# A third of a wide projection moved into the mLSTM cell, in steps between the cell's own matmuls

## The reference, cut to what matters

```python
proj = x @ w_in                      # (512, 1024) @ (1024, 4*768 + 12 + 256)
q, k, v = heads of proj[:, 0:768], proj[:, 768:1536] * 128**-0.5, proj[:, 1536:2304]
o_gate  = proj[:, 2304:3072]
# per head and chunk c (128 positions), with the state before the chunk:
s   = (q @ k.T) * exp(d - m)                       # 128 x 128, causal
num = s @ v + w_inter * (q @ c_prev)               # and den likewise
h   = num / max(|den|, exp(-m))
c_new = decay * c_prev + (w * k).T @ v
h   = (h - mean) * rsqrt(var + eps) * norm_g       # per head
out = sigmoid(o_gate) * h
y   = concat([out, h_mem]) @ w_out                 # then LayerNorm, router, experts
```

## Time and profile before

| | us |
|---|---|
| time, median of 3 | 1474.45 |
| the profiled execution, its own time | 1475.07 |
| its span | 1473.1 |
| PE busy (matmul) | 1350.9, 92% |
| PE weight loads | 724.1, 49% |
| DVE busy | 504.1, 34% |
| ACT busy | 287.8, 20% |
| mLSTM cell | from 866.3 to 932.4 |

### The profile page before, as it was taken

One profiled execution on the slowest core, in us unless ns is written; L12 is line 12 of the kernel. 1 busy time (PEld: TensorE's weight loads), 2 busy tenths in 40 slices (PEclk: granted clock), 3 DMA queues, 4 the chain that ended last, 5 costly groups with the idle time before them and its releaser, 6 DMA issues. The chain is left out here.

```text
span 1473.1 us, 16175 instructions
## 1 busy us (share of the span) xinstructions
PE 1350.9 (92%) x6590; PEld 724.1 (49%) x6590; DVE 504.1 (34%) x1042; ACT 287.8 (20%) x507; POOL 39.1 (3%) x64
## 2 busy tenths in 40 slices
PE   6999899999999899988999986698999999989885
PEld 5878683333333333325677875585333333333331
DVE  3264683123122122123543328575122122121221
ACT  3231340011011011012532212431011011010111
POOL 1000000000000000000000000000000000000000
PEclk9999999999999999999999998799999999999998
DMA  8320759999999999997133042249999999999994
GB/s 361 157 86 1 318 209 420 426 428 428 427 425 427 427 428 427 428 427 291 58 115 115 0 189 97 86 160 406 427 427 427 427 427 427 427 427 428 428 427 185
DMA packets 39628, 465.85 MB, mean 316 GB/s; under 512 B 6400, under 2 KB 6528, under 8 KB 12160
## 3 DMA queue, kind: packets, MB, share of 16 engines
q1 hardware_dynamic: 34656, 455.33, 73.6%
q0 software_dynamic: 4608, 8.40, 1.5%
q10 hardware_dynamic: 288, 1.05, 0.2%
HBM read 460.55 MB, written 12.58 MB: 321 GB/s over the span
## 5 line engine op out<-in xcount | busy, mean ns | idle before, releaser
L1054 PE MATMUL bank<-ring,xT 128*64 128x512 f32 x2048 | 460.4, 596 | 44.7 <-DMA ring<-in_w_pack 44.4
L1054 PEld LDWEIGHTS bank<-ring,xT 128*64 128x64 f32 x2048 | 149.0, 137 | 311.5 <-issue 311.2
L1093 PE MATMUL bank<-ring,pad 128*64 128x512 f32 x1024 | 237.7, 606 | 7.1 <-DVE pad L1275 3.2
L1265 DVE COPY xT<-bank 128x512 f32<-128x512 f32 x60 | 41.5, 691 | 442.5 <-PE bank L1040 442.5
L1093 PEld LDWEIGHTS bank<-ring,pad 128*64 128x64 f32 x1024 | 69.2, 138 | 165.7 <-issue 152.8
L1186 ACT ACTIVATE pad<-bank 128x256 f32<-128x256 f32 x64 | 24.5, 383 | 460.0 <-PE bank L1054 460.0
L1192 ACT COPY pad<-bank 128x512 f32<-128x512 f32 x64 | 37.4, 585 | 346.3 <-PE bank L1093 346.3
L1275 DVE COPY pad<-bank 128x256 f32<-128x256 f32 x64 | 27.0, 423 | 179.7 <-PE bank L1068 179.7
L1040 PEld LDWEIGHTS bank<-x_sb 128*128 128x128 f32 x480 | 58.1, 191 | 49.0 <-issue 45.4
L451 PE MATMUL bank<-x_half_hi,w_half_hi 128*128 128x512 f32 x160 | 64.0, 400 | 11.5 <-DVE x_half_lo L506 11.5
L1110 PE MATMUL bank<-pad,x_sb 64*128 64x512 f32 x256 | 72.3, 641 | 1.4 <-ACT pad L1192 1.4
(11 more groups left out here) (264 smaller groups left out, 1436.7 us busy)
## 6 DMA issues: line engine op xcount, KB each, us to landing
ring<-in_w_pack SPq DMA_DIRECT2D x190, 2048.0 KB, 35.0
ring<-in_mlstm_w_in SPq DMA_DIRECT2D x6, 2048.0 KB, 7.3
ring<-in_conv_slabs SPq DMA_DIRECT2D x6, 1536.0 KB, 10.2
ring<-in_w_out SPq DMA_DIRECT2D x2, 4096.0 KB, 12.3
ring<-in_w_kv_mem SPq DMA_DIRECT2D x2, 2048.0 KB, 26.2
ring<-in_w_pack SPq DMA_DIRECT2D x4, 1024.0 KB, 41.0
x_rows<-x_sb SPq DMA_DIRECT2D x6, 512.0 KB, 2.6
ring<-in_xT SPq DMA_DIRECT2D x4, 512.0 KB, 8.3
```

The lines of the kernel that those rows point to most:

```text
L1054: last = nc.tensor.matmul(GU_BANK[e % 2][64 * f:64 * f + 64, :], xgT[e // 2 % 2][:, 4 * h + c, 64 * (e % 2):64 * (e % 2) + 64], gu[:, c, f ...
L1093: last = nc.tensor.matmul(Y_BANK[e % 2][64 * n:64 * n + 64, :], hidT[e % 2][:, c, 64 * f:64 * f + 64], dn[:, f, c, 512 * n:512 * n + 512], ...
L1265: V.tensor_copy(xgT[q % 2][:, 4 * h:4 * h + 4, :], o[:, :].rearrange("p (c r) -> p c r", c=4)).then_inc(xcopied, 1)
```

## The change

The third group of wide pieces (8 to 11) leaves the projection's script. The pieces 8 to 10 are still split there, by ACT and DVE, into the four places; the last, piece 11, is split at the start of the cell. The cell then computes the 512 gate columns tile by tile: the tile of chunk c in eight steps of three matmuls into bank 7, put at hand-chosen places between the cell's own matmuls (`open_gates(n)` issues the next n steps; 6 + 5 + 9 + 8 + 4 over the stretches before chunk 0 and in chunks 0 to 3), and ACT takes the Sigmoid of each finished tile. Since bank 7 is taken, the state product and the turned output use bank 6 alone, three heads at a time, and the second three wait until the first three are read. x's high half must live through the cell, so the working tiles move from xT to R0. w_out's place holds x's low half and split weights, so its load waits for the last step; of the experts' units only one is loaded in the cell, behind the last raw weights, and units 1 and 2 follow with unit 3 after the cell.

```diff
-EARLY = (0, 3)
+EARLY = (0, 1)
...
-                flat = xT[:, :, :].rearrange("p k s -> p (k s)")
-                cell = lambda i, n: flat[:, i * 784:i * 784 + ML_HEADS * n].rearrange("p (h d) -> p h d", h=ML_HEADS)
+                cell = lambda i, n: R0[:, 4096 + i * 784:4096 + i * 784 + ML_HEADS * n].rearrange("p (h d) -> p h d", h=ML_HEADS)
...
-                script += [("wide", i) for i in range(2, 12)]
+                script += [("wide", i) for i in range(2, 8)]
                 pieces = [st for st in script if st[0] not in ("S", "T", "V", "cols")]
+                pieces += [("wide", i) for i in range(8, 12)]
+                IN_CELL = len(pieces) - 1
...
-                    if st in pieces and pieces.index(st) + 3 < len(pieces):
+                    if st in pieces and pieces.index(st) + 3 < IN_CELL:
...
                 @block.sync
                 def _(sp):
-                    sp.dma_start(w_out_sb, w_out[1]).then_inc(in_w_out[1], 16)
+                    sp.wait_ge(w_lo, 1)
                     for n in range(EARLY[1]):
                         load_unit(sp, 1, n)
+                    sp.wait_ge(o_done, N_CHUNKS)
+                    sp.dma_start(w_out_sb, w_out[1]).then_inc(in_w_out[1], 16)
...
+                    def open_gates(n):
+                        for _ in range(n):
+                            c, k = o_steps.pop(0)
+                            if c and k == 0:
+                                pe.wait_ge(o_out, c)
+                            if c == 0 and k == 6:
+                                pe.wait_ge(w_lo, 1)
+                            hi, lo = (by_2(a)[:, k % 2, :] for a in o_half[k // 2])
+                            z = slice(c * P, (c + 1) * P)
+                            for w, xh in ((hi, x_hi), (hi, x_lo), (lo, x_hi)):
+                                last = nc.tensor.matmul(bank[7][:, :], xh[:, k, z], w, start=(k == 0 and w is hi and xh is x_hi),
+                                                        stop=(k == KT - 1 and w is lo))
+                            if k == KT - 1:
+                                last.then_inc(o_done, 1)
...
                         last.then_inc(spread, 1)
+                        open_gates(fill[0])
...
                         last.then_inc(scored, 1)
+                        open_gates(fill[1])
...
+                    def turn_out(c, fill):
                         pe.wait_ge(h_ready, c + 1)
+                        for i in range(2):
+                            if i == 0 and c < N_CHUNKS - 1:
+                                pe.wait_ge(inter_read, 2 * c + 2)
+                            else:
+                                pe.wait_ge(h_out, 2 * c + i)
+                            for j in range(3):
+                                last = nc.tensor.transpose(third(P)[:, j, :], hh[:, 3 * i + j, :], ident[:, :])
+                            last.then_inc(h_turned, 1)
+                            if i == 0:
+                                open_gates(fill)
+
+                    front(0, (0, 2))
+                    open_gates(4)
...
+                            for i in range(2):
+                                if i:
+                                    pe.wait_ge(inter_read, 2 * c - 1)
+                                elif c > 1:
+                                    pe.wait_ge(h_out, 2 * (c - 1))
+                                for j in range(3):
+                                    last = nc.tensor.matmul(third(HD)[:, j, :], qT[:, 3 * i + j, z], state[:, 3 * i + j, :],
+                                                            start=True, stop=True)
+                                last.then_inc(inter, 1)
+                                if i == 0:
+                                    open_gates(1)
...
                         if c < N_CHUNKS - 1:
-                            front(c + 1)
+                            front(c + 1, ((2, 4, 3)[c], 0))
+                            open_gates((3, 2, 2)[c])
+                        else:
+                            open_gates(3)
                         if c:
-                            turn_out(c - 1)
-                    turn_out(N_CHUNKS - 1)
+                            turn_out(c - 1, (2, 2, 0)[c - 1])
+                    turn_out(N_CHUNKS - 1, 0)
...
+                    def gate(c):
+                        act.wait_ge(o_done, c + 1)
+                        nc.scalar.activation(ogate[:, c, 256:768], bank[7][:, :], ACT.Sigmoid).then_inc(o_out, 1)
...
+                    nc.scalar.copy(by_2(o_half[3][0]), last_raw).then_inc(w_hi, 1)
                     weights(0)
                     for c in range(N_CHUNKS):
                         if c < N_CHUNKS - 1:
                             weights(c + 1)
+                        gate(c)
...
-                            dve.wait_ge(inter, c)
                             for i in range(2):
-                                last = V.tensor_tensor(three(qC, i), pair(6, HD)[i], col(c, W_COL, i, HD), ALU.mult)
-                            last.then_inc(inter_read, 1)
-                            dve.wait_ge(inter_read, c)
+                                dve.wait_ge(inter, 2 * c - 1 + i)
+                                V.tensor_tensor(three(qC, i), third(HD), col(c, W_COL, i, HD), ALU.mult).then_inc(inter_read, 1)
+                            dve.wait_ge(inter_read, 2 * c)
...
+                        dve.wait_ge(o_out, c + 1)
                         V.tensor_tensor(hh[:, :, :], hh[:, :, :], ogate[:, c, :].rearrange("p (h d) -> p h d", h=ML_HEADS),
...
                     weigh_scores(0)
+                    dve.wait_ge(w_hi, 1)
+                    V.tensor_tensor(by_2(o_half[3][1]), last_raw, by_2(o_half[3][0]), ALU.subtract).then_inc(w_lo, 1)
```

More of the change, by code:

```diff
@@ L1612, in mlstm_phase @@
                 results, ends = [], []
-                for i, (kind, n) in enumerate(pieces):
+                for i, (kind, n) in enumerate(pieces[:-4]):
                     if kind != "wide":
@@ L1619, in mlstm_phase @@
                     else:
-                        banks = ((2, 3, 4, 6), (0, 1, 5, 7), (2, 3, 4, 6))[n // 4]
-                        results += [(("v", "vo", "o")[n // 4], t, banks[t], n // 4 > 0) for t in range(TT)]
+                        banks = ((2, 3, 4, 6), (0, 1, 5, 7))[n // 4]
+                        results += [(("v", "vo")[n // 4], t, banks[t], n // 4 > 0) for t in range(TT)]
                         ends.append(ends[-1] + TT)
@@ L1626, in ended @@
                     what, n = results[m][0:2]
-                    if what in ("v", "vo", "o"):
-                        return ends[pieces.index(("wide", 4 * ("v", "vo", "o").index(what) + 3))] - TT + n + 1
+                    if what in ("v", "vo"):
+                        return ends[pieces.index(("wide", 4 * ("v", "vo").index(what) + 3))] - TT + n + 1
                     return ends[pieces.index((what, n))]
@@ L1868, in cell_phase @@
             HD = ML_DH + 1
+            last_piece, last_raw = d["split_in_cell"]
+            o_half = [w1_half[(last_piece - 3 + q) % 4] for q in range(4)]
+            by_2 = lambda a: a[:, :].rearrange("p (k n) -> p k n", k=2)
             s = lambda n: sem("p5_" + n, ph)
+            w_hi, w_lo, o_done, o_out = s("w_hi"), s("w_lo"), s("o_done"), s("o_out")
             spread, compared, exped, weighed = s("spread"), s("compared"), s("exped"), s("weighed")
@@ L1874, in cell_phase @@
             scored = s("scored")
+            third = lambda w: bank[6][:, 0:3 * w].rearrange("p (h d) -> p h d", h=3)
             pair = lambda b, w: [bank[b + i][:, 0:3 * w].rearrange("p (h d) -> p h d", h=3) for i in range(2)]
@@ L1879, in _, with front @@
                 def _(sp):
-                    sp.dma_start(w_out_sb, w_out[1]).then_inc(in_w_out[1], 16)
+                    sp.wait_ge(w_lo, 1)
                     for n in range(EARLY[1]):
                         load_unit(sp, 1, n)
+                    sp.wait_ge(o_done, N_CHUNKS)
+                    sp.dma_start(w_out_sb, w_out[1]).then_inc(in_w_out[1], 16)
                 @block.tensor
                 def _(pe):
-                    def front(c):
+                    x_hi, x_lo = x2_half
+                    o_steps = [(c, k) for c in range(N_CHUNKS) for k in range(KT)]
+                    def open_gates(n):
[12 more added lines that the diff above has]
+                                last.then_inc(o_done, 1)
+                    def front(c, fill):
                         z = slice(c * P, (c + 1) * P)
@@ L1919, in _ @@
                         if c:
-                            if c > 1:
-                                pe.wait_ge(h_out, 2 * (c - 1))
                             pe.wait_ge(state_ready, c)
[L1923 to L1926, removed]
+                            for i in range(2):
[9 more added lines that the diff above has]
+                                    open_gates(1)
                         pe.wait_ge(weighed, c + 1)
@@ L1948, in write_out @@
```

(7 more changed lines are left out.)

20 lines of the change are left out of this document (5 added, 15 removed).

## The result

The changed kernel takes 1462.64 us (median of 4, 1459.14 to 1464.1) beside 1475.18 (1474.31 to 1476.44): ratio 0.9911, 95% interval 0.989 to 0.9932, 12.5 us less (the kernel before was measured a fourth time; 1474.45 was the median of the first three). 1461 was forecast. The profiled execution has 1464.1 us, span 1462.2, so it is 11.0 under the one of before (1475.07).

What follows compares the result with a forecast made beforehand. PE was taken to bound the wide projection, and DVE with waits between DVE, PE and ACT the cell. 1475.07 - 21.7 + 8 = 1461.4, beside the median 1460.8, so 1461 us; range 1456 to 1469.

Steps and rivals of the forecast that it cites:

- The removal: Wide projection: 96 matmuls at 0.227 us leave PE's path, a gain of 21.7 us ahead of the cell.
- The cell: mLSTM cell: the added steps and the shared bank lengthen it by 7.6 us, taken as 8.
- the walk: Cell's PE, DVE and ACT queues followed chunk by chunk at assumed prices; last heads written at 73.7 instead of 66.1.
- The parts ahead: Stages before the cell: positions as before except the removed matmuls, so the block ends at about 844.3.
- SP's queue: Loads: w_out lands at cell time 73.0, covered by 1.6 us; units 1 and 2 behind the cell cost nothing.
- Tables: ScalarE in the cell: a table load before the Sigmoid costs 1.28 us alone, nothing else paid.
- drain of about 1.38: ScalarE rule left out of the sum: the two gating Sigmoids some 2.8 us later in all, 1464 instead of 1461.
- (a): Rival, PE's clock in the cell: at mean 0.8 costs 9.5 us more, 1470; chance 0.20 up to the old time.
- (b): Rival, cell: steps hide fully, growth only the bank's serial waits, 2.7 us, so 1455.5; chance 0.10.
- (c): Rival, output projection: w_out lands late, start up to 2 us later, 1463; lies in the forecast's own range.
- (d): Rival, expert stage: bound by loads, so the gain is not passed on; 1474.5 + 8 at worst; chance 0.01.
- the signs named: Trace checks: cell starting at 844.6, span about 74 us, w_out within 2 us of its reader, later work 13 to 14 earlier.

Runs made afterwards that it cites:

- e1: Kernel before with the third group of wide pieces left out altogether (gate columns constant, their slab not loaded): 1453.91 us, ratio 0.9846.
- e7: Changed kernel with w_out's load held back until the last gated tile is ready: 1470.14 us, ratio 0.9957.
- e3: Changed kernel with only 4 of its 32 gate steps, every wait and Sigmoid kept: 1464.76 us, ratio 0.9922.
- e2: Kernel before, gates still in the projection, with state product and turned output in halves in bank 6 alone: 1483.18 us, ratio 1.0054.
- e4: Changed kernel with the state product's second half in bank 0, turned output whole in banks 4 and 5, some steps moved: 1454.76 us, ratio 0.9863.
- e5: e9 plus 40 filler matmuls on constants while PE is idle around the cell's end: 1452.61 us, ratio 0.9835.
- e10: Changed kernel with only the turned output moved whole to banks 4 and 5, steps between its halves put behind it: 1459.35 us, ratio 0.9884.
- e8: Changed kernel with no unit of the experts loaded in the cell, units 0 to 3 all after it: 1464.14 us, ratio 0.9921.
- e6: Changed kernel with Exp in place of Sigmoid for the cell's gate columns, so no table load between them: 1461.8 us, ratio 0.9905.
- e9: e4 with one step moved from the last chunk to the end of the chunk before: 1453.09 us, ratio 0.9846.
- e12: e4 with w_out loaded in two halves of 2 MB, without fillers: 1454.04 us, ratio 0.9851.
- e11: e4 with w_out loaded in two halves of 2 MB and the 40 fillers of e5: 1451.61 us, ratio 0.9835.

## Why the prediction was right, and where not

**The removal** (21.7): right, 21.4 by e1.

**The cell** (+7.6, taken as 8): every wait of the walk is in the trace; +9.85 in this execution. DVE reaches the three state products, and the cell its end, at these cell times:

| | first | second | third | end | first scores |
|---|---|---|---|---|---|
| before | 20.14 | 33.54 | 48.51 | 66.08 | 1.60 |
| the walk | 21.4 | 38.7 | 55.7 | 73.7 | 1.5 |
| changed | 22.55 | 39.48 | 56.35 | 75.93 | 2.63 |
| e7 (same cell) | 20.95 | 37.87 | 54.73 | 73.96 | 1.61 |
| e3 (4 steps) | 20.46 | 37.35 | 54.19 | 75.48 | 1.60 |
| e2 (no steps) | 20.16 | 37.17 | 54.12 | 75.52 | 1.60 |
| e4 (three banks) | 22.51 | 36.98 | 50.12 | 66.07 | 2.93 |

The walk missed the clock at either end of the cell. At the start, the scores and the first two steps at the low clock cost 1.6 (the changed kernel beside e7). At the end, behind the last steps, PE is at the low clock again: the last stage takes 19.6 where the walk had 18.0, and four halves of a turned output at 0.90 in place of 0.49, each in series with ACT, are 1.6. In between the walk was too long, by 0.5 to 1.0 at e7's positions, and that hid a part: e7's end agrees with the walk to 0.3 because two errors cancel, which is luck. So the term was 2 us too small.

**What I ascribed the growth to** was wrong in part, though the sum held. The walk charged chunk 0's two steps, the four steps of chunk 1 and the Sigmoids, and gave the bank a part. Compare the rows that start alike. e2 has the growth without any step (9.4). From one state product to the next, e2, e3 and e7 take the same 16.8 to 17.0 us: the steps of chunks 1 and 2 cost nothing. In chunk 0 they cost 0.5 (20.95 beside 20.46), and in the last chunk they give 2.1 back (19.2 us beside 21.3), because PE does the last chunk's work at the full clock: the last intra takes 1.50 in place of 2.54. So the bank's serial halves are the whole growth, and the steps end 1.5 us ahead. e4 shows the same from the other side. My own sum for e2 failed in the same place: I walked it at the full clock, 71.5, and it was 75.5, as PE without steps ran at 0.78.

**The parts ahead**: not quite as before. PE's last matmul of the projection started at 844.59, where 843.24 was due. Of these 1.35, 0.39 stand ahead of the layer's projection (its first matmul at 702.33, at 701.94 before) and 0.96 in its first 20 us (19.80 to the first attention product, 18.84 before). This stretch had clock 0.79 in this execution and 0.90 in the one of before. It is an accident of the execution and no effect of the change: kernels with the same code up to there had 0.79 (e5, e10), 0.90 (seven others) and 1.00 (e3, 17.30 us), and e1 and e2, with the code of before, had 0.79:

```profile
698.50:715.00 16.50, 12.67 (x45) 7.53 (x46) 7.42 (x10) 6.30 (x9) 2.26 (x4) 0.79 0.34 129
```

Together: -21.76 + 1.35 + 9.85 - 0.8 (the first half of the output projection, 24.05 in place of 24.86, which the sum did not have) = -11.4; measured -11.27, the 0.1 lying between the stages. Over the runs it is 12.5, where 13.7 was forecast. Of the signs named, these missed: the cell's start (844.6 forecast, 845.98), w_out within 2 us of its reader (3.1), and everything behind 13 to 14 earlier (11.3). A step took 0.69, and 0.80 behind matmuls of another kind, where 0.68 was taken.

**SP's queue**: right. w_out was covered by 3.1 (1.6 walked), and e7 shows that past the cover each us counts (7.9, with 8 expected); the late units cost nothing that the runs can tell (e8). **Tables**: a load takes 1.28, starts 0.02 after the Exp and ends 0.01 before the Sigmoid. Taking the load away from both waits moved the chain by 1.4 (e6). By the Trainium skill's drain of about 1.38 with every switch (ScalarE: Activation LUTs, "What ACT_TABLE_LOAD costs") 2.8 us more would have been lost; the trace does not agree.

**Rivals.** (a) came true only at the two ends of the cell, for 1.6 us each, and not for the 9.5 that it priced. In the middle the clock rose, from stretches of 0.62 and 0.70 to 1.00, across PE's waits of 0.7 to 1.2 us between the groups. The Trainium skill's swinging clock (TensorE: Matmul & The Clock Gate, "A second HAM failure mode: psum-queue depth-cycling"), by which a PE that idles briefly between groups of matmuls swings between the levels, is not seen in the middle of the changed kernel's cell. e3 does swing, between 0.50 and 1.00 with 0.78 as its mean over 20 us, with PE's waits of 1.6 and 3.3; the only difference is the 28 steps, so they are what keeps the changed kernel out of it. (b) had the steps right and the bank wrong: the steps did hide, but the bank's serial waits cost 9.4 and not 2.7. e4's 1454.76 is near (b)'s 1455.5 because it has no such waits. (c) became true only once the cell was shorter (w_out late by 0.6 in e4, 0.2 in e9). (d) fell with e1.

## What to carry to other kernels

Work moved into another engine's shadow costs where it stands in its own engine's order; walk that order. Ask first for the bank that it takes: here the moved work was free and the buffer that others gave up for it cost 9.4 us, until free times of three other banks were used. Here the work in PE's gaps also kept its clock up, so taking it out gained nothing (e3). And compare stages only between executions that enter them at the same clock.

## What the runs showed of the hardware

Removing 19 us of PE work left the cell no shorter (75.48 in e3, beside 75.93, and 73.96 in e7, which starts like e3). The cell's first scores took 2.4 to 2.9 us in nine executions and 1.6 in five; among the kernels made from the changed one both occur with the same code ahead (e3, e7 and e12 beside the rest). Runs of one kernel differ by 5 us (1459.14 to 1464.1). The clock at the cell's start (1.6) and at the projection's start (1.0 between 0.79 and 0.90, 2.5 between 0.79 and 1.00) could make 2.6 to 4.1 of these; this is an estimate, as one run of each kernel has a trace. It fits that the two runs at 1464 had a mean granted clock of 0.982, those at 1461.4 and 1459.1 had 0.985 and 0.986. Forty fillers (ones times zeros, in bf16) held the granted clock at 1.00 from the last step to the projection's first matmul in e5 and e11 (0.66 in e9, 0.67 in e12).
